# Turning the identity on TensorE where it stands idle, in a hybrid encoder kernel

## The chip, the cores and the metric

The kernel runs on one core of a Trainium2 chip (trn2). A core has a matrix engine, TensorE (PE; its weight loads are listed as PEld), VectorE (DVE), ScalarE (ACT), GpSimd (POOL) and SyncE (SP), which issues most transfers; each takes its own queue of instructions in order, and they meet through semaphores. SBUF is the on-chip memory, PSUM (8 banks of 512 fp32 columns on 128 partitions) takes what TensorE computes. The metric is device microseconds of one execution.

## The reference

Two encoder layers on 1024 tokens of 1024 channels, all in float32, batch 1.

```
x = (1, 1024, 1024)
layer 0: hn = rms_norm(x, g0); u = hn @ ev_w_in            # 1024 x 3072
         y_att = differential attention (4 heads, q/k norm, partial rotary) of u[:, :1536]
         y_hy  = order-2 Hyena of u[:, 1536:]  (3-tap conv, long filters by FFT, gating)
         x = x + concat(y_att, y_hy) @ ev_w_out
layer 1: u = rms_norm(x, g1) @ od_w_in                     # q, k, v, o, gates
         y = bidirectional chunkwise mLSTM (4 heads, chunks of 128), rms_norm, * sigmoid(o)
         x = x + y @ od_w_out
each layer: xt = rms_norm(x, gf)
         top-1 of 4 groups, top-2 of 8 experts in it;  32 experts, d_expert 512
         x = x + sum over picked e of gate * (silu(xt @ w1[e]) * (xt @ w3[e])) @ w2[e]
```

## The kernel before, in words

The program is a row of phases, each a block in which every engine has its own instruction list; at the end of a phase all engines meet at a barrier (`end_phase`), so nothing of the next phase starts before all of them are through. In order: `first_norm` (normalise x, turn it into xnT), `attention_project`, `attention`, `hyena_project`, `hyena_filter`, `hyena_transform`, `out_route` of layer 0 (output projection, residual, norm, router), `experts`, `overflow`, `renorm`, `ml_project_qk`, `ml_project_vo`, `ml_gates`, `ml_scan`, `out_route` of layer 1, `experts`, `overflow`.

Large products run as three fp32r products, high x high, high x rest and rest x high (`split_product`, lines 193 to 195): ScalarE casts the high part, VectorE subtracts it to get the rest (`rest_of`, line 188). Weights come in chunks of 2 MB through a ring of three slots; a phase finds its first chunks already there. So at the start of a projection phase TensorE first waits for these splits: `attention_project` for x and the first half of a weight chunk (waits on `x_rest` and `w_rest`), `hyena_project` and `ml_project_qk` for a 128-column weight block and a quarter of x, `out_route` for a quarter of w and half of y. Then it runs through tiles of 128 tokens (or blocks of 128 columns) with 8 contraction steps each.

`hyena_filter` has two small fp32 products of the filter network (line 1510) and four turnings (line 1520) per round, eight rounds; VectorE multiplies each result with a decay (lines 1584, 1586) that ScalarE computes, and its chain goes on to a sum that GpSimd gathers. Its first products need nothing that is computed in the phase.

`out_route` (line 658) is built once per layer. In layer 1 (`hs` is given) TensorE first turns the normalised mLSTM output (`turn_y`, line 849): the first half, then, when VectorE has read it (`y_rest`), the second; in layer 0 `turn_y` does nothing. After the last tile, `logits(NT - 1)`, the router's selection is a long chain on VectorE (lines 1129 to 1226) with two short parts on TensorE in it: a count of places, nine products that wait for `picked` and release `placed` (lines 905, 908), and sixteen products that write the list of tokens per block, wait for `marked` in two halves of eight and release `listed` (line 916). VectorE reads the lists (line 1224), GpSimd then gathers the first two blocks of tokens by an indirect transfer (line 831).

`experts` (line 1833) runs over the 32 experts, one block of 128 tokens each. For a block, TensorE turns the gathered tokens (`turn_x`, line 2002, eight turnings into banks 0 and 1), ScalarE casts them (`xgH`, line 2071), VectorE subtracts (`xgL`, line 2119), and only then does `one(e)` begin its products (lines 1985 to 1993). On ScalarE the order is written out: first half of the first weight chunk, the cast of the turned tokens, then the next halves; VectorE follows it. A ring slot is refilled when VectorE has made both rests of its chunk.

`renorm` (line 2316) loads x again, normalises each tile of 128 tokens on ScalarE and VectorE and turns it (line 2399).

Of the kernel before, what the change touches and what calls it, by code (L numbers as in the profile page):

```python
# [14 lines left out]
P = 128  # L15
# [56 lines left out]
def build(nc, I, out):  # L72
    ctx = ExitStack()
    with ctx:
# [111 lines left out]
        def rest_of(out, whole, high):  # L186

            return nc.vector.tensor_tensor(out, whole, high.bitcast(F32), ALU.subtract)  # L188

        def split_product(dst, lhs, rhs, start, stop):  # L190


            nc.tensor.matmul(dst, lhs[0], rhs[0], start=start, stop=False)  # L193
            nc.tensor.matmul(dst, lhs[0], rhs[1], start=False, stop=False)  # L194
            return nc.tensor.matmul(dst, lhs[1], rhs[0], start=False, stop=stop)  # L195
# [87 lines left out]
        def attention_project(q, kH, kL, v):  # L283
# [3 lines left out]
            with ExitStack() as st:  # L287
# [15 lines left out]
                with nc.Block() as block:  # L303
# [8 lines left out]
                    @block.tensor  # L312
                    def _(pe):
                        def turn(i):
                            pe.wait_ge(normed, i + 1)
                            if i >= 2:
                                pe.wait_ge(qk_moved, i - 1)
                            if i >= NT + 2:
                                pe.wait_ge(k_rest, i - NT - 1)
                            for h in range(AH):  # L320
                                last = nc.tensor.transpose(psum[:, 4 + i % 2, h * P:(h + 1) * P],
                                                           qn[:, i % 3, h * P:(h + 1) * P], ident[:])
                            last.then_inc(turned, 1)

                        for i in range(3 * NT):
                            c, j = divmod(i, NT)
                            pe.wait_ge(x_rest, i + 1)
                            if i >= 4:
                                if i - 4 < STEPS:
                                    pe.wait_ge(qk_read, i - 3)  # L330
                                else:
                                    pe.wait_ge(v_copied, i - 3 - STEPS)
                            for k in range(KD):
                                if j == 0 and k % 4 == 0:
                                    pe.wait_ge(w_rest, 2 * c + k // 4 + 1)
                                last = split_product(psum[:, i % 4, :], (xH[:, i % 2, k, :], xL[:, i % 2, k, :]),
                                                     (wH[:, c % 2, k, :], wide_rest(S_ATT + c)[:, k, :]),
                                                     k == 0, k == KD - 1)
                            last.then_inc(proj, 1)
                            if 2 <= i <= STEPS + 1:  # L340
                                turn(i - 2)
# [316 lines left out]
        def out_route(name, yT, hs, head_gain, s0, xsrc, xdst, layer, slots, slot_gate, ctrl, xg):  # L658
# [6 lines left out]
            with ExitStack() as st:  # L665
# [103 lines left out]
                with nc.Block() as block:  # L769
# [68 lines left out]
                    def _(pe):  # L838
# [38 lines left out]
                        def logits(j):  # L877
# [7 lines left out]
                                                        start=(k == 0), stop=(k == KD - 1))  # L885
                            last.then_inc(logit_ok, 1)

                        turn_y(0, 0)
                        turn_y(0, 1)
                        for j in range(NT):  # L890
                            project(j, 0)
                            turn_y(j + 1, 0)
                            if j:
                                turn_x(j - 1)
                            project(j, 1)
                            turn_y(j + 1, 1)
                            if j:
                                logits(j - 1)
# [2 lines left out]

                        pe.wait_ge(picked, 1)
                        nc.tensor.matmul(psum[:, PB, 0:(NT + 1) * NE], upperR[:], both[:].rearrange("p j e -> p (j e)"),
                                         start=True, stop=False)
# [3 lines left out]
                                                    start=False, stop=(j == NT - 1))  # L910
                        last.then_inc(placed, 1)

                        for n in range(16):
                            if n % 8 == 0:
                                pe.wait_ge(marked, n // 8 + 1)
                            last = nc.tensor.matmul(psum[:, SB, 0:3 * NBLKP], A[:, n, :],
                                                    B[:, n, :, :].rearrange("p f b -> p (f b)"),
                                                    start=(n == 0), stop=(n == 15))
                        last.then_inc(listed, 1)

                    @block.scalar
                    def _(act):
# [308 lines left out]
        def hyena_project(z, yT, xnH, o, gain, post, hidden, consts):  # L1231
# [4 lines left out]
            with ExitStack() as st:  # L1236
# [40 lines left out]
                with nc.Block() as block:  # L1277
# [12 lines left out]
                    def _(pe):  # L1290
# [9 lines left out]
                        def hidden_layer(u):  # L1300
# [4 lines left out]
                            else:  # L1305
# [3 lines left out]
                            nc.tensor.matmul(psum[:, TURN + u % 2, :], w[:], x[:, piece(u)], start=True, stop=True  # L1309
                                             ).then_inc(lin, 1)  # L1310

                        for i in range(STEPS):
                            pe.wait_ge(w_rest, i + 1)
                            if i >= 3:
                                pe.wait_ge(padded, i - 2)
                            for half in range(2):
                                ts = slice(half * 512, (half + 1) * 512)
                                for k in range(KD):
                                    if i == 0 and k % 4 == 0:
                                        pe.wait_ge(x_rest, 2 * half + k // 4 + 1)  # L1320
                                    last = split_product(psum[:, 2 * (i % 3) + half, :],
                                                         (wH[:, i % 2, k, :], block_of(wide_rest, i)[:, k, :]),
                                                         (xnH[:, k, ts], xnL[:, k, ts]), k == 0, k == KD - 1)
                            last.then_inc(proj, 1)
                            if i < NT:
                                turn(i)
                            if MLP <= i < MLP + 4:
                                hidden_layer(i - MLP)
# [153 lines left out]
        def hyena_filter(z, zT, hidden, consts, hs, hd, hinv, tab):  # L1482
# [4 lines left out]
            with ExitStack() as st:  # L1487
# [6 lines left out]
                with nc.Block() as block:  # L1494
# [7 lines left out]
                    def _(pe):  # L1502
# [11 lines left out]
                        def turn(n):  # L1514
# [6 lines left out]
                                                           z[:, ct, t0:t0 + 4 * P - 3:4], ident[:])  # L1521
                            last.then_inc(turned, 1)

                        for n in range(NT):
                            filters(n)
                            turn(n)
# [306 lines left out]
        def experts(layer, slots, slot_gate, ctrl, total, xg, y, yidx, oidx, w_over):  # L1833
# [6 lines left out]
            with ExitStack() as st:  # L1840
# [50 lines left out]
                with nc.Block() as block:  # L1891
# [85 lines left out]
                    def _(pe):  # L1977
# [63 lines left out]
                        def tail():  # L2041
                            turn_hid(LAST)
                            out(0, LAST, LAST + 1, 0)

                        turn_x(0, 0, 0)
                        for e in range(4):
                            one(e // 2, e % 2, e)
                        with pe.Fori(2, NE // 2 - 1) as i:
# [267 lines left out]
        def renorm(src, gain):  # L2316
# [3 lines left out]
            with ExitStack() as st:  # L2320
# [6 lines left out]
                with nc.Block() as block:  # L2327
                    @block.sync
                    def _(sp):
                        for j in range(NT):  # L2330
                            sp.dma_start(x_all[:, j, :], rows[:, j, :]).then_inc(x_in[j], 16)
                            if j == 0:
                                sp.dma_start(g_bc[:], gain.partition_broadcast(P)).then_inc(gain_in, 16)
# [56 lines left out]

                    @block.tensor
                    def _(pe):
                        for j in range(NT):
                            pe.wait_ge(xn_ok, j + 1)
                            if j >= 4:
# [33 lines left out]
        def ml_project_qk(qkT, G, xnH):  # L2429
# [3 lines left out]
            with ExitStack() as st:  # L2433
# [19 lines left out]
                with nc.Block() as block:  # L2453
# [6 lines left out]

                    @block.tensor
                    def _(pe):
                        for i in range(CONV):
                            pe.wait_ge(w_rest, i + 1)
                            if i >= 4:
# [689 lines left out]
```

## Time and profile before

| | us |
|---|---|
| median of 3 runs | 2720.84 (2719.23 to 2721.32) |
| profiled execution, its own time | 2724.51 |
| its span, first to last instruction | 2722.5 |
| TensorE busy | 2428.2 (89%), 11788 matrix instructions |
| VectorE busy | 1827.1 (67%) |
| ScalarE busy | 1452.7 (53%) |
| GpSimd busy | 483.5 (18%) |
| mean granted TensorE clock | 0.938 |

The profile is of one execution. Busy shares are means over phases with different limits, so each phase has to be read by itself. The granted clock is given as a share of full speed, 2.4 GHz; 0.50 is the lower of its two levels, 1.2 GHz.

### The profile page before, as it was taken

To read this page: it belongs to the slowest core of one execution; us is meant where nothing else is said; L and a number is where in the kernel's file an instruction comes from. 1 tells how busy PE (TensorE), PEld (TensorE's weight loads), DVE (VectorE), ACT (ScalarE), POOL (GpSimd) and SP (SyncE) were. 2 spreads that over 40 slices of the span, in tenths; PEclk is the share of its full clock that TensorE was granted. 3 is DMA by queue.
4 is the path that set the end of the run, shared out by engine and by line. 5 is a ranking of instruction groups with operands and counts; after the bars stand their busy time and mean duration, and the time that the engine had idled before them with its cause. 6 is when DMAs were issued, how large, how long until landed. Compare 5 with 4: busy or idle time off the path is not lost. (4 is left out here: it accounts for less than half of the span.)

```text
span 2722.5 us, 32997 instructions
## 1 busy us (share of the span) xinstructions
PE 2428.2 (89%) x11788; PEld 1995.0 (73%) x11788; DVE 1827.1 (67%) x2083; ACT 1452.7 (53%) x1776; POOL 483.5 (18%) x433
## 2 busy tenths in 40 slices
PE   5989989796959999999948999779695999999995
PEld 4768877585857888888836888667584888888882
DVE  5748856578358998899835301078546988888980
ACT  4337842322227887788834212146423778887870
POOL 0001100100002332333200000025200323332310
PEclk9999999897979999999978999979796999999997
DMA  4010011101339999999980101200424999999994
GB/s 171 31 64 1 1 39 42 70 31 36 117 115 344 389 385 381 382 389 391 373 327 22 50 31 64 91 1 1 144 109 170 387 367 380 369 387 380 395 375 167
DMA packets 85787, 542.51 MB, mean 199 GB/s; under 512 B 18870, under 2 KB 22551, under 8 KB 59704
## 3 DMA queue, kind: packets, MB, share of 16 engines
q1 hardware_dynamic: 64232, 503.11, 47.0%
q0 software_dynamic: 19008, 33.61, 5.1%
q10 hardware_dynamic: 2448, 4.46, 0.4%
q8 instruction: 63, 1.03, 0.2%
q14 instruction: 36, 0.29, 0.0%
HBM read 521.70 MB, written 55.05 MB: 212 GB/s over the span
## 5 line engine op out<-in xcount | busy, mean ns | idle before, releaser
L2119 DVE TENSOR_TENSOR wL<-ring,wH 128x2048 fp32r<-128x2048 f32 x384 | 869.1, 2288 | 153.7 <-ACT wH L2066 148.4
L2066 ACT CAST wH<-ring 128x2048 fp32r<-128x2048 f32 x384 | 730.3, 1910 | 216.6 <-DMA ring<-in_moe_w 158.8
L1985 PE MATMUL psum<-wH,xgH 128*128 128x512 f32 x1024 | 408.0, 398 | 14.0 <-DVE xgL L2119 13.9
L1987 PE MATMUL psum<-wH,xgL 128*128 128x512 f32 x1024 | 401.3, 392 | 0.0
L1993 PE MATMUL psum<-wL,xgH 128*128 128x512 f32 x1024 | 275.4, 391 | 0.0
L1985 PEld LDWEIGHTS psum<-wH,xgH 128*128 128x128 f32 x1024 | 193.6, 189 | 57.3 <-DVE xgL L2119 13.0
L1993 PEld LDWEIGHTS psum<-wL,xgH 128*128 128x128 f32 x1024 | 193.0, 188 | 40.7
L1987 PEld LDWEIGHTS psum<-wH,xgL 128*128 128x128 f32 x1024 | 193.8, 189 | 38.4
L1985 PE MATMUL psum<-wH,hidH 128*128 128x512 f32 x512 | 207.8, 406 | 11.0 <-DVE hidL L2119 11.0
L1987 PE MATMUL psum<-wH,hidL 128*128 128x512 f32 x512 | 201.6, 394 | 0.0
L1932 POOL COPY gidx<-slots 128x1 int32 (+1 forms) x60 | 62.6, 1044 | 488.6 <-PE psum L2002 488.6
L1993 PE MATMUL psum<-wL,hidH 128*128 128x512 f32 x512 | 138.0, 392 | 0.0
L195 PE MATMUL psum<-xn_high,ring_rest 128*128 128x512 f32 x320 | 126.7, 396 | 0.0
L1985 PEld LDWEIGHTS psum<-wH,hidH 128*128 128x128 f32 x512 | 97.5, 190 | 30.5 <-DVE hidL L2119 11.4
L1993 PEld LDWEIGHTS psum<-wL,hidH 128*128 128x128 f32 x512 | 97.1, 190 | 20.4
L1987 PEld LDWEIGHTS psum<-wH,hidL 128*128 128x128 f32 x512 | 97.7, 191 | 18.5
L193 PE MATMUL psum<-w_high_route_rest,y_high_route 128*128 128x512 f32 x256 | 104.5, 408 | 7.0 <-DVE ring_rest L188 7.0
L193 PE MATMUL psum<-w_high_vo,xn_high 128*128 128x512 f32 x256 | 102.1, 399 | 3.6 <-DVE ring_rest L188 3.6
L195 PE MATMUL psum<-w_high_vo,xnT_rest 128*128 128x512 f32 x256 | 101.9, 398 | 0.0
L194 PE MATMUL psum<-ring_rest,xn_high 128*128 128x512 f32 x256 | 101.6, 397 | 0.0
L194 PE MATMUL psum<-ring_rest,y_high_route 128*128 128x512 f32 x256 | 101.4, 396 | 0.0
L195 PE MATMUL psum<-w_high_route_rest,y_rest_route 128*128 128x512 f32 x256 | 101.4, 396 | 0.0
(425 smaller groups left out, 4728.9 us busy)
## 6 DMA issues: line engine op xcount, KB each, us to landing
ring<-in_moe_w SPq DMA_DIRECT2D x192, 2048.0 KB, 9.4
ring<-in_ev_w_in SPq DMA_DIRECT2D x6, 2048.0 KB, 14.7
xnT<-in_moe_w SPq DMA_DIRECT2D x6, 2048.0 KB, 13.8
ring<-in_od_w_in SPq DMA_DIRECT2D x6, 2048.0 KB, 15.4
xn_scratch<-xn_route SPq DMA_DIRECT2D x16, 512.0 KB, 2.6
ow<-in_moe_w SPq DMA_DIRECT2D x3, 2048.0 KB, 22.6
x_all<-in_x SPq DMA_DIRECT2D x4, 1024.0 KB, 8.1
ring<-in_ev_w_out SPq DMA_DIRECT2D x2, 2048.0 KB, 7.8
```

Source lines behind the costliest of these rows:

```text
L193: nc.tensor.matmul(dst, lhs[0], rhs[0], start=start, stop=False)
L194: nc.tensor.matmul(dst, lhs[0], rhs[1], start=False, stop=False)
L195: return nc.tensor.matmul(dst, lhs[1], rhs[0], start=False, stop=stop)
L1932: nc.gpsimd.tensor_copy(idx[:, b:b + 1], slots[:, bass.ds(e, 1)]).then_inc(idx_ok, 1)
L1985: nc.tensor.matmul(psum[:, bank, :], xh[:, k, :], w3[0][:, n, cols], start=(half == 0 and n == 0), stop=False)
L1987: nc.tensor.matmul(psum[:, bank, :], xl[:, k, :], w3[0][:, n, cols], start=False, stop=False)
L1993: ins = nc.tensor.matmul(psum[:, bank, :], xh[:, k, :], w3[1][:, n, cols], start=False, stop=(half == 1 and n == len(ks) - 1))
L2066: nc.scalar.copy(half_of(wH, b, e, c, half), raw(e, c, half)).then_inc(w_high, 1)
L2119: return nc.vector.tensor_tensor(out, whole, high.bitcast(F32), ALU.subtract)
```

## The change

A new helper, `idle_products(bank, n)`, turns the 128x128 identity n times into the first 128 columns of a PSUM bank. Nothing reads the result. It has no semaphore, and n is fixed when the program is built. It is called at twelve lines of TensorE's lists; two of them are inside `experts` and three in `out_route` that both layers run, so an execution passes eighteen calls with 869 turnings in all: one each of 55 (`attention_project`), 52 (`hyena_project`), 30 (`hyena_filter`), 50 (`renorm`) and 55 (`ml_project_qk`); 45 and 26 in each `experts`; in `out_route` 52 (layer 0) or 120 and 45 (layer 1), and in both layers 50, 72 and 12. Nothing is removed or moved.

```
+        def idle_products(bank, n):
+
+            for _ in range(n):
+                nc.tensor.transpose(psum[:, bank, 0:P], ident[:], ident[:])

@@ attention_project
+                        idle_products(7, 55)
                         for i in range(3 * NT):
@@ out_route
+                        idle_products(3, 52 if hs is None else 120)
                         turn_y(0, 0)
                         turn_y(0, 1)
+                        if hs is not None:
+                            idle_products(3, 45)
                         for j in range(NT):
                             project(j, 0)
...
+                        idle_products(3, 50)
                         pe.wait_ge(picked, 1)
...
                         last.then_inc(placed, 1)

+                        idle_products(3, 72)
                         for n in range(16):
...
                         last.then_inc(listed, 1)
+                        idle_products(3, 12)
@@ hyena_project
+                        idle_products(7, 52)
                         for i in range(STEPS):
@@ hyena_filter
+                        idle_products(7, 30)
                         for n in range(NT):
                             filters(n)
@@ experts
+                        idle_products(7, 45)
                         turn_x(0, 0, 0)
+                        idle_products(7, 26)
                         for e in range(4):
                             one(e // 2, e % 2, e)
@@ renorm
+                        idle_products(7, 50)
                         for j in range(NT):
@@ ml_project_qk
+                        idle_products(7, 55)
                         for i in range(CONV):
```

## Rows read from the trace of the kernel before

**Rows 1.** The page, parts 1 (PE alone) and 2 (TensorE's clock, tenths in 40 slices).
```profile
PE 2428.2 (89%) x11788; PEld 1995.0 (73%) x11788; DVE 1827.1 (67%) x2083; ACT 1452.7 (53%) x1776; POOL 483.5 (18%) x433
...
PEclk9999999897979999999978999979796999999997
```

**Rows 2.** Stretches at four stage starts: start:end, us, PE busy, granted clock, DMA.
```profile
34.81:40.13 5.32, 0.00 (x1) 0.50 0.12 32
40.13:44.70 4.57, 4.57 (x11) 0.50 0.03 9
349.55:354.87 5.32, 0.00 (x1) 0.72 0.46 129
354.87:358.72 3.85, 3.85 (x9) 0.50 0.24 82
663.84:666.81 2.97, 0.00 (x0) 0.50 0.68 210
666.81:672.74 5.93, 5.93 (x14) 0.50 1.00 246
1441.49:1446.81 5.32, 0.00 (x0) 0.50 0.37 114
1446.81:1450.98 4.17, 4.17 (x10) 0.50 0.00 0
...
348.22:349.55 1.33, 0.00 (x0) 1.00 0.00 0
```

**Rows 3.** First norm: one line's durations (min/median/max ns); timeline (start, us, count).
```profile
L273 PE MATMUL psum<-ident,x_all x64: 272/273/476, 19.1 to 32.9; 128*128 128x128 f32 x64
...
19.13 3.65 PE L273 MATMUL psum<-ident,x_all 128*128 128x128 f32 x16 [19.13 <-DVE x_all L257]
...
23.04 1.64 PE L273 MATMUL psum<-ident,x_all 128*128 128x128 f32 x8 [0.27 <-DVE x_all L257]
...
24.84 1.09 PE L273 MATMUL psum<-ident,x_all 128*128 128x128 f32 x8 [0.15 <-DVE x_all L257]
```

**Rows 4.** Start of the experts: timeline of layer 0, slow stretches of both layers.
```profile
810.36 1.94 PE L2002 MATMUL psum<-ident,xg 128*128 128x128 f32 x8 [7.70 <-PEq L105]
...
815.81 0.80 PE L1985 MATMUL psum<-wH,xgH 128*128 128x512 f32 x1 [3.51 <-DVE xgL L2119]
...
815.81:819.52 3.71, 3.71 (x9) 0.50 0.61 138
2086.75:2092.70 5.95, 5.95 (x14) 0.50 0.67 191
```

**Rows 5.** Sum of forty stretches of 5 us, 1000 to 1200, inside the first experts.
```profile
sum 200.00, PE 199.21 PEld 165.23 DVE 177.92 ACT 158.93 POOL 66.23; mean PE 4.98 PEld 4.13 DVE 4.45 ACT 3.97 POOL 1.66
```

**Rows 6.** Start of layer 1's out_route: PE's stretches and a timeline row.
```profile
1911.51:1923.52 12.01, 0.00 (x1) 0.50 0.88 288
1932.29:1935.68 3.39, 3.39 (x10) 0.50 0.32 124
...
1930.79 0.68 DVE L188 TENSOR_TENSOR y_rest_route<-psum,y_high_route 128x512 fp32r<-128x512 f32 x1
```

**Rows 7.** Start of hyena_filter, timeline.
```profile
504.01 2.10 PE L1510 MATMUL psum<-hy_w,hy_hidden 64*128 64x512 f32 x4 [5.50 <-PEq L105]
...
509.16 0.69 DVE L1584 TENSOR_TENSOR xnT<-psum,hy_decay 128x512 f32<-128x512 f32 x1 [1.74 <-PE psum L1510]
```

**Rows 8.** The router's selection in layer 0: PE's stretches and a timeline row.
```profile
780.61:787.59 6.98, 0.00 (x0) 0.50 1.02 383
789.72:798.98 9.26, 0.00 (x1) 0.50 0.03 11
...
802.70 0.21 DVE L1224 TENSOR_SCALAR slots<-psum 128x48 int32<-128x48 f32 x1 [1.05 <-PE psum L916]
```

**Rows 9.** PE's stretches: start of renorm, end of the router.
```profile
1411.43:1423.56 12.13, 0.00 (x0) 0.50 0.84 329
802.67:810.36 7.69, 0.00 (x0) 0.50 0.25 68
```

More of the change, by code:

```diff
@@ L188, in rest_of, with idle_products @@
             return nc.vector.tensor_tensor(out, whole, high.bitcast(F32), ALU.subtract)
+        def idle_products(bank, n):
+            for _ in range(n):
+                nc.tensor.transpose(psum[:, bank, 0:P], ident[:], ident[:])
         def split_product(dst, lhs, rhs, start, stop):
@@ L323, in turn @@
                             last.then_inc(turned, 1)
+                        idle_products(7, 55)
                         for i in range(3 * NT):
@@ L886, in logits @@
                             last.then_inc(logit_ok, 1)
+                        idle_products(3, 52 if hs is None else 120)
                         turn_y(0, 0)
                         turn_y(0, 1)
+                        if hs is not None:
+                            idle_products(3, 45)
                         for j in range(NT):
@@ L900, in _ @@
                         logits(NT - 1)
+                        idle_products(3, 50)
                         pe.wait_ge(picked, 1)
@@ L911, in _ @@
                         last.then_inc(placed, 1)
+                        idle_products(3, 72)
                         for n in range(16):
@@ L919, in _ @@
                         last.then_inc(listed, 1)
+                        idle_products(3, 12)
                     @block.scalar
@@ L1310, in hidden_layer @@
                                              ).then_inc(lin, 1)
+                        idle_products(7, 52)
                         for i in range(STEPS):
@@ L1522, in turn @@
                             last.then_inc(turned, 1)
+                        idle_products(7, 30)
                         for n in range(NT):
@@ L2043, in tail @@
                             out(0, LAST, LAST + 1, 0)
+                        idle_products(7, 45)
                         turn_x(0, 0, 0)
+                        idle_products(7, 26)
                         for e in range(4):
@@ L2392, in _ @@
                     def _(pe):
+                        idle_products(7, 50)
                         for j in range(NT):
@@ L2462, in _ @@
                     def _(pe):
+                        idle_products(7, 55)
                         for i in range(CONV):
```

## The prediction

> **What bounds the kernel now.** The page's first two parts come first [rows 1]: TensorE (PE) is busy 89% of the span, and its granted clock is at 0.9 or more in most of the 40 slices and at 0.7 in a few. The next view is the table of stretches, cut at each stage: it shows that low slices are stage starts. In [rows 2] each stage that opens with fp32r products has the same two halves. For 2.97 to 5.32 us the engine has nothing to do, since ScalarE and VectorE still split the first operands; the products then run at granted clock 0.50 (1.2 of the two levels, 1.2 and 2.4 GHz) for 3.85 to 5.93 us before the clock goes to 1.00. In these stages PE is busy without a gap afterwards, so a microsecond of products at the low clock costs half a microsecond of the total. The reader should see both numbers side by side: the idle time is the cover that the new work has, half of the slow time is all that it can win. The expert loops are also PE's: 199.21 of 200 us busy in the middle of the first [rows 5]. The router's selection is VectorE's chain, with PE idle for 6.98 and 9.26 us inside it [rows 8].
>
> **What one added operation costs.** The change only adds: 869 transposes of the identity over an execution, waiting for nothing, in order ahead of the stage's own work on PE's queue. Whatever stands behind them on that queue waits until they are done. The trace has the same form, a 128x128 fp32 transpose against the identity, in the first norm [rows 3]. Slow: 16 took 3.65 us with 0.476 for a single one, so one follows another after (3.65 - 0.476)/15 = 0.212 us. Fast: 8 took 1.09 with 0.272 for one, so (1.09 - 0.272)/7 = 0.117 us. These lengths also decide what the clock did there: the page gives 1.00 for the first norm, but the first 16 have the slow length and the later ones the fast one. So transposes alone raise the clock, here between 23.04 and 24.84 us, some 4 to 5.7 us after they began. (The Trainium skill says otherwise: "TensorE: Matmul & The Clock Gate", section "PE-mode transpose", holds that the full clock does not engage for them. The trace disagrees, with 0.476 against 0.272 us; by that rule the change would have nothing but cost, and that is a rival below.)
>
> How long N of them take: the slow phase of the six stage starts in [rows 2, 4] is 4.57, 3.85, 5.93, 4.17, 3.71 and 5.95, mean 4.7 us. That is 22 transposes at 0.212, the rest at 0.117: D(55) = 8.6, D(52) = 8.2, D(50) = 8.0, D(45) = 7.4, D(30) = 5.6 us. With the clock up from the start it is 0.117 N. The cover is often shorter than that.
>
> **Part by part.** Net cost = what overruns the cover, less half of the slow stretch.
> - attention_project, 55: 8.6 - 5.32 = 3.3 late, half of 4.57 won: +1.0 us. If the clock does not fall between the stages: 6.4 - 5.32 - 2.3 = -1.2.
> - ml_project_qk, 55: 8.6 - 5.32 - 2.1 = +1.2 (other end -1.0).
> - hyena_project, 52: here the clock is still 1.00 when the stage begins, 1.33 us after the last product [rows 2], and it fell only in the long pause that the transposes now fill. So 6.1 - 5.32 - 1.9 = -1.1 (other end: 8.2, +1.0).
> - out_route of layer 0, 52: cover only 2.97. 8.2 - 2.97 - 2.97 = +2.3 (other end +0.2).
> - experts, 45 before the first turning and 26 after it, in both layers: PE starts together with the others at 810.36, with its operand landed, so there is no cover at all for the 45 [rows 4]. ScalarE's copy of the turned operand waits for it, behind that its next weight casts, and behind those VectorE's. First product after 7.4 + 8 x 0.117 + 26 x 0.117 = 11.4 us where it was 815.81 - 810.36 = 5.45: 5.95 late; won 1.86 and 2.98. +4.1 and +3.0, together +7.1. The loop behind it is PE's [rows 5] and takes over the delay. Ends: 5.3 for the 45 gives +2.9 in all; if the refill of the ring, which hangs on the later casts, counted rather than PE, up to 7 each.
> - out_route of layer 1, 120 and 45: 120 take 4.7 + 98 x 0.117 = 16.2 us against 12.01 idle; but the result of the first turning is read by VectorE only at 1930.79 [rows 6], and 1911.51 + 16.2 + 0.5 = 1928.2 is before that. Hidden; if that cover were gone, 4.2. The 45 after the second turning have none: the first product followed it at once. 5.3 to 7.4 us, depending on whether the clock lasted over the pause before; I take the middle, 6.4, less half of 3.39: +4.7.
> - hyena_filter, 30: the first product comes with the stage, again no cover. Two rounds ended at 509.16, 5.15 us after the start and at the low clock [rows 7]; at the high one they are half. 5.6 + 2.6 - 5.15 = +3.1; behind them VectorE's chain starts late by that (ends +0.9 and +4).
> - Router, both layers: 50 against 6.98 idle, 8.0 - 6.98 = 1.0 late; the nine small products behind them filled 787.59 to 789.72, 2.1 us at the low clock, and win that back. 72 at 0.117 = 8.4 fit into 9.26. The 16 list products then end sooner, and the 1.05 us that VectorE waits for them at the end [rows 8] goes: -1.05 twice, -2.1. What is late next is VectorE itself. If the clock falls in between: 4.7 + 50 x 0.117 = 10.5, 1.3 late: +0.2 each.
> - renorm, 50, under 12.13 us of waiting for data, and the 12 at the router's end under 7.69 [rows 9]: 0. Without cover they would be 8.0 and 1.4 to 2.5 each. The pause that is left behind renorm's 50 is 4 us, so I count on no gain for its own transposes (at most 1 us).
>
> Sum: 1.0 + 1.2 - 1.1 + 2.3 + 7.1 + 4.7 + 3.1 - 2.1 = +16.2 us. The profiled execution took 2724.51 us (span 2722.5, 2.0 around it), 3.7 above the median; against it the changed one would be 2740.7, and in terms of the median 2720.84 + 16.2 = 2737.0.
>
> **The rivals.**
> (a) Faster: two transposes of one and the same operand follow each other quicker than those of fresh data, say a load of weights hidden under the last product, at half the distance, 0.106 and 0.0585. Then D(N) = 2.35 + 0.0585 N: 5.6 for 55, 5.0 for 45. Same working: -2.0, -1.9 (both projections), -1.9 (hyena), -0.6, experts 5.0 + 0.9 + 1.5 - 5.45 = 2.0 late, so +0.1 and -1.0, layer-1 route +2.1, filter +1.5, router -2.1: -5.8, 2715. The sum changes sign at about 0.073 us for one at the high clock. For it: the small covers at the projections would just fit. Against it: all transposes that the trace shows have 0.117. 11%.
> (b) The clock stays up over the pauses between stages, since PE is now idle for 1 to 2 us there only: 0.117 N everywhere. -1.2, -1.0, -1.1, +0.2, +2.9, 5.3 - 1.7 = +3.6, +0.9, -2.1: +2.2, 2723. For it: 1.33 us did not lower it; against it: at most of the ten starts it is 0.50 already when the stage begins. 10%.
> (c) The transposes don't raise the clock: 0.212 N, nothing won. 6.3 + 5.7 + 6.3 + 8.0, experts 9.5 + 1.9 + 5.5 - 5.45 = 11.5 twice, layer-1 route 16, filter 6.4, router (3.6 + 6.0) twice: +91, 2812. Against it: [rows 3]. 4%.
> (d) The experts' end is set by the stream of weights and their late start is absorbed: 16.2 - 7.1 = +9, 2730. Against it: PE has 0.4% of idle time in that stretch. 10%.
>
> **How the numbers follow.** Forecast 2737, 62%, its own range 2728 to 2746 from the ends above; 3% for none of these. 2717 to 2749 leaves out (a), (c) and part of the tails, some 2 in 10. Faster or slower by 0.2% is 5.4 us, about what a measurement can tell from no change: (a) lies on that edge, with more favourable ends 8% are below 2715.4; (b), part of (a) and the low end of (d) make 15% within; 77% slower.
>
> **What would show it.** In the changed profile: the added operations stand 0.21, then 0.117 us apart (0.106 and 0.06 for (a)); first products in attention_project at 43 instead of 40.13, in out_route of layer 0 some 5 us later in its stage, the first experts' product 11.4 us behind the stage's start and at clock 1.00; VectorE's wait of 1.05 us for the lists gone. Wrong would be: products at 0.50 after the transposes, or no overrun, or an expert loop whose end does not move with its start.

## The result and the profile after

The changed kernel took 2732.37 us (median of 8 runs, 2726.89 to 2736.69), the kernel before on the same chip 2721.08 us (2719.23 to 2724.61): a ratio of 1.0039, 95% interval 1.0027 to 1.0051, or +11.3 us. Run again beside other kernels in a later series it gave 2727.05 us and 1.0018 (1.0009 to 1.0026), +5.4 us. Slower both times; on record were 2737 us and +16.2 us. Both results are inside the stated 2717 to 2749 us, the second a little below the forecast's own range of 2728 to 2746, and the forecast was 5 and 11 us too much.

Parts 1 (busy time of each engine) and 2 (TensorE's busy share in tenths, and its clock, in 40 slices) of the page of after, against [rows 1]:

```profile
PE 2515.0 (92%) x12657; PEld 2088.3 (76%) x12657; DVE 1827.8 (67%) x2083; ACT 1451.4 (53%) x1776; POOL 468.8 (17%) x433
...
PE   6989999796989999999969999779898999999995
...
PEclk9999999898999999999979999979999999999998
...
L193 PE MATMUL psum<-ident 128*128 128x128 f32 x869 | 121.4, 311 | 46.6 <-PEq L105 46.6
```

The last row is from part 5: the 869 turnings are busy for 121.4 us, and each call starts as soon as TensorE's list comes to it. The clock rose as meant (mean 0.961 instead of 0.938, of 2.4 GHz), TensorE's busy share went from 89 to 92%, and the span grew from 2722.5 to 2731.4 us.

The calls at six stages, in the timeline of after (start, us, engine, line, operation, count; in brackets the wait before), against [rows 2, 4, 6, 7]:

```profile
34.82 6.19 PE L193 MATMUL psum<-ident 128*128 128x128 f32 x55 [1.71 <-PEq L105]
40.77 0.48 PE L198 MATMUL psum<-w_high_qk,x_high_qk 128*128 128x512 f32 x1
...
497.69 6.22 PE L193 MATMUL psum<-ident 128*128 128x128 f32 x30 [5.51 <-PEq L105]
503.84 1.25 PE L1523 MATMUL psum<-hy_w,hy_hidden 64*128 64x512 f32 x4
505.14 0.69 DVE L1598 TENSOR_TENSOR xnT<-psum,hy_decay 128x512 f32<-128x512 f32 x1 [8.42 <-PE psum L1523]
...
507.00 0.69 DVE L1598 TENSOR_TENSOR xnT<-psum,hy_decay 128x512 f32<-128x512 f32 x1 [0.57 <-PE psum L1523]
...
661.70 8.54 PE L193 MATMUL psum<-ident 128*128 128x128 f32 x52 [4.03 <-PEq L105]
670.00 0.47 PE L198 MATMUL psum<-w_high_route_rest,y_high_route 128*128 128x512 f32 x1
...
808.58 7.73 PE L193 MATMUL psum<-ident 128*128 128x128 f32 x45 [5.44 <-PEq L105]
816.14 1.04 PE L2016 MATMUL psum<-ident,xg 128*128 128x128 f32 x8
816.78 1.07 ACT L2087 CAST xgH<-psum 128x512 fp32r<-128x512 f32 x2 [6.33 <-PE psum L2016]
817.02 3.00 PE L193 MATMUL psum<-ident 128*128 128x128 f32 x26
...
819.78 0.47 PE L1999 MATMUL psum<-wH,xgH 128*128 128x512 f32 x1
...
1442.77 9.16 PE L193 MATMUL psum<-ident 128*128 128x128 f32 x55 [1.70 <-PEq L105]
1451.68 0.48 PE L198 MATMUL psum<-xn_high,w_high_ml 128*128 128x512 f32 x1
...
1915.92 15.22 PE L193 MATMUL psum<-ident 128*128 128x128 f32 x120 [4.31 <-PEq L105]
...
1936.38 6.74 PE L193 MATMUL psum<-ident 128*128 128x128 f32 x45
1942.88 0.48 PE L198 MATMUL psum<-w_high_route_rest,y_high_route 128*128 128x512 f32 x1
```

All first products behind calls now take 0.47 or 0.48 us, a full-clock length, where [rows 4] has 0.80. And nearly all of them start the moment the last turning ends: the engine still turns the identity when the operands are already there. That is the overrun. The 55 turnings took 6.19 us at the first stage and 9.16 us at ml_project_qk; the same list of operations has two lengths.

Stage lengths, from the first instruction of each stage to that of the next, for the profiled executions of before, after, and after again (its span 8.4 us shorter than the first), with the term on record:

| stage | before | after | again | change, on record | change, seen |
|---|---|---|---|---|---|
| attention_project | 155.15 | 152.27 | 152.24 | +1.0 | -2.9, -2.9 |
| attention | 159.58 | 157.51 | 157.83 | 0 | -2.1, -1.8 |
| hyena_project | 154.44 | 153.08 | 153.07 | -1.1 | -1.4, -1.4 |
| hyena_filter | 30.33 | 34.49 | 34.52 | +3.1 | +4.2, +4.2 |
| out_route and router, layer 0 | 146.50 | 146.88 | 147.04 | +1.25 | +0.4, +0.5 |
| experts, layer 0 | 601.09 | 604.41 | 601.95 | +4.1 | +3.3, +0.9 |
| ml_project (to the gates) | 312.02 | 314.58 | 312.97 | +1.2 | +2.6, +1.0 |
| out_route and router, layer 1 | 169.80 | 171.55 | 167.75 | +3.65 | +1.8, -2.1 |
| experts, layer 1, to the end | 641.22 | 643.98 | 642.22 | +3.0 | +2.8, +1.0 |

The stages left out changed by 1.5 us or less. The -2.9 and -2.1 of the first two rows are not the calls' work alone: two test kernels with nothing changed in these two stages have them 2 us shorter each as well (experiment 2). A stage of one execution is not a measurement: the last one, whose beginning was as before in four of the test kernels below (the one with the router's calls, with the three uncovered ones, with the three large ones, with attention_project's alone), had 644.30, 639.03, 641.36 and 641.90 us there. For sizes the timed series below count.

### The profile page after: what moved, and what is told of

Its sections match the earlier page's. It is cut to its first block and busy times, and to the rows that moved or that the text cites. A ratio compares the mean times of both kernels' runs of the same rounds, so it can differ in the third digit from the quotient of the medians.

```text
span 2731.4 us, 34735 instructions
## 1 busy us (share of the span) xinstructions
PE 2515.0 (92%) x12657; PEld 2088.3 (76%) x12657; DVE 1827.8 (67%) x2083; ACT 1451.4 (53%) x1776; POOL 468.8 (17%) x433
## 5 line engine op out<-in xcount | busy, mean ns | idle before, releaser
L2135 DVE TENSOR_TENSOR wL<-ring,wH 128x2048 fp32r<-128x2048 f32 x384 | 869.5, 2288 | 153.0 <-ACT wH L2082 148.5
L193 PE MATMUL psum<-ident 128*128 128x128 f32 x869 | 121.4, 311 | 46.6 <-PEq L105 46.6
L193 PEld LDWEIGHTS psum<-ident 128*128 128x128 f32 x869 | 117.9, 164 | 49.3 <-issue 49.3
L1946 POOL COPY gidx<-slots 128x1 int32 (+1 forms) x60 | 49.8, 829 | 494.9 <-PE psum L2016 494.9
L1999 PEld LDWEIGHTS psum<-wH,hidH 128*128 128x128 f32 x512 | 97.6, 191 | 30.4 <-DVE hidL L2135 11.3
```

Of the source, the lines that this page charges most:

```text
L193: nc.tensor.transpose(psum[:, bank, 0:P], ident[:], ident[:])
L1946: nc.gpsimd.tensor_copy(idx[:, b:b + 1], slots[:, bass.ds(e, 1)]).then_inc(idx_ok, 1)
L1999: nc.tensor.matmul(psum[:, bank, :], xh[:, k, :], w3[0][:, n, cols], start=(half == 0 and n == 0), stop=False)
```

## Experiments

Twelve test runs were made, two of them repeats, in three series, each beside runs of the kernel before on its chip (medians 2721.36, 2721.66 and 2720.99 us). In the expectations attproj is attention_project, and x4_fitted the kernel of experiment 9. The theory is the sum of the prediction: a call costs what it overruns its cover and wins half of the slow stretch.

**1. The change without the experts' calls**

```
-                        idle_products(7, 45)
                         turn_x(0, 0, 0)
-                        idle_products(7, 26)
```

> The change without its two calls in experts (45 and 26 left out, both layers); all other calls stay. Theory (the turnings have no cover there and the expert loop is TensorE's, so the late start is passed on): in both profiles of before and after the experts' first product moved from 5.45 to 11.4 us and 10.3 us behind the stage's start, so the time falls by about 7 us against the change, to 2725, ratio to before 1.0015. Rival (the stream of weights sets the end of the experts and absorbs the late start): no change, 2732, ratio 1.004.

Measured: 2722.30 us, ratio 1.0001 (0.9989 to 1.0013). (The trace of after has the first products 11.2 and 10.1 us behind the stage's start.) Against the first series of the change, 1.0039 (1.0027 to 1.0051), the experts' calls cost more than nothing; against its second, 1.0018 (1.0009 to 1.0026), the intervals overlap, so this run alone does not show it. It does show that what is left costs less than on record: the other terms, +9.1 together on record, are within 3.5 us of nothing.

**2. The experts' calls alone**, in both layers, in the kernel before

```
+                        idle_products(7, 45)
                         turn_x(0, 0, 0)
+                        idle_products(7, 26)
```

> The kernel before with only the change's two calls in experts (45 before the first turning, 26 after it). Theory: +7 us over before (4.1 and 3.0, bounds 3 and 8), ratio 1.0026, and the whole of each experts stage longer by 3 to 4 us, from its first instruction to the next stage's. Rival (absorbed): 0, ratio 1.000.

Measured: 2725.65 us, ratio 1.0016 (1.0003 to 1.0029), so +4.4 us where the sum has +7.1. The delay is real. Its profiled execution spans 2722.6 us, no longer than before, with the stages 605.17 and 642.89 (before 601.09 and 641.22) but attention_project and attention each 2 us shorter though nothing in them was changed. One profile would have hidden the cost. What makes those two shorter can be seen in one stretch of attention_project, first of before, then of this kernel (start:end, length, PE busy, granted clock, DMA share, GB/s):

```profile
109.55:112.96 3.41, 3.22 (x10) 0.50 0.00 0
...
109.53:112.94 3.41, 3.41 (x18) 1.00 0.00 0
```

At the same place the clock was down in one execution and up in the other, with 10 and 18 products done. The fourteen profiled executions fall into two groups: in eight the clock goes down near 109 us and attention takes 159.5 to 159.7 us (before among them), in six it does not and attention takes 157.2 to 157.8 (after and after again among them, this kernel and that of experiment 5, where no call stands in or before these stages). The kernel of experiment 9 is in one group the first time and in the other the second time.

**3. The same with a longer first call**

```
-                        idle_products(7, 45)
+                        idle_products(7, 90)
                         turn_x(0, 0, 0)
```

> The kernel with the experts' calls alone (45 and 26), the 45 made 90. Theory (the first product is late by every added transpose, at 0.117 us each once the clock is up, and nothing later absorbs it): 45 x 0.117 = 5.3 us in each layer, +10.5 us over the kernel with 45, so 2736 and a ratio near 1.0055. Rival (the experts' weights come by DMA and a late start is won back behind it): the same as with 45, a ratio of 1.0016.

Measured: 2738.82 us, ratio 1.0063 (1.0050 to 1.0076), 12.8 us (give or take 5) above the kernel with 45. Layer 0 in the timelines of the two, first 45, then 90:

```profile
805.44 8.07 PE L193 MATMUL psum<-ident 128*128 128x128 f32 x45 [7.38 <-PEq L105]
...
816.98 0.48 PE L1992 MATMUL psum<-wH,xgH 128*128 128x512 f32 x1
```

```profile
811.15 12.86 PE L193 MATMUL psum<-ident 128*128 128x128 f32 x90 [7.61 <-PEq L105]
...
827.48 0.47 PE L1992 MATMUL psum<-wH,xgH 128*128 128x512 f32 x1
```

45 more turnings are 4.79 us more, 0.106 each on average, and the first product goes from 11.54 to 16.33 us behind the stage's start; in layer 1 from 10.98 to 15.83. That is 9.6 us over both, inside the interval of 7.8 to 17.8 us by which the total grew. The rival in which the stream of weights absorbs a late start is out. (In the two single profiles the experts' stages differ by 3.5 and 2.0 us only, 608.66 and 644.92 against 605.17 and 642.89; what took up the rest there was not followed.)

**4. The router's calls alone**, in both layers, in the kernel before

```
+                        idle_products(3, 50)
                         pe.wait_ge(picked, 1)
...
+                        idle_products(3, 72)
                         for n in range(16):
...
                         last.then_inc(listed, 1)
+                        idle_products(3, 12)
```

> The kernel before with only the router's calls (50, 72 and 12, both layers). Theory: the list products end sooner, VectorE's wait of 1.05 us for them goes, in each layer; the 50 are 1 us late and the nine products win it back: -2.1 us in all, 2719, ratio 0.9992; bounds -2.1 and +0.4. Rival (the late 50 and the gap between the calls cost more than is won): VectorE waits over 1 us longer for the places, +1 to +3 us, ratio 1.0007.

Measured: 2721.33 us, ratio 1.0003 (0.9992 to 1.0014): +0.8 us, from -2.2 to +3.8. Nothing that can be measured, in either direction. The mechanism itself is there. VectorE's write of the lists in after, which in [rows 8] waited 1.05 us, waits no more:

```profile
800.85 0.20 DVE L1236 TENSOR_SCALAR slots<-psum 128x48 int32<-128x48 f32 x1
```

and in the router-only kernel the two stages that hold a router are 144.81 and 168.37 us, 1.7 and 1.4 less than before. These 3 us are at the edge of what the series can tell, and its last stage happened to be 3.1 us longer.

**5. The uncovered calls outside the experts alone**, in the kernel before

```
+                        idle_products(3, 52 if hs is None else 0)
                         turn_y(0, 0)
                         turn_y(0, 1)
+                        if hs is not None:
+                            idle_products(3, 45)
...
+                        idle_products(7, 30)
                         for n in range(NT):
                             filters(n)
```

> The kernel before with three calls alone, those outside the experts for which the terms of the sum were late starts: 30 at hyena_filter, 52 at the start of the first out_route, and in the second out_route 45 behind the turning (no 120 ahead of it). Theory of the sum (a run of calls that outlasts its cover delays the stage, and half of the slow stretch comes back): +3.1 +2.3 +4.7 = +10, so 2731.5 and a ratio near 1.0037. In the change's own trace the hyena_filter stage is 4.2 us longer than before. Rival (the calls fill time in which TensorE would have waited anyway): +3 at most, a ratio of 1.001 or less.

Measured: 2726.29 us, ratio 1.0020 (1.0010 to 1.0029): +5.4 us (2.7 to 7.9) instead of +10.1. They cost, about half as much. Its stages that hold them are 3.6, 1.8 and 3.7 us longer than before, together 9.1, close to the sum; but hyena_transform (behind hyena_filter, unchanged) was 3.5 us shorter, and 9.1 - 3.5 = 5.6 us is what the timed runs have. The whole stage in before, in this kernel and in that of experiment 6, then one stretch of it in before and the same one, 32.67 us behind the stage's start, in this kernel (start:end, length, PE busy, granted clock, DMA share, GB/s):

```profile
534.26:663.82 129.56, 105.87 (x448) 0.88 0.05 17
...
533.13:659.16 126.03, 102.37 (x448) 0.91 0.06 17
...
531.51:658.82 127.31, 103.65 (x448) 0.89 0.05 17
...
566.93:573.76 6.83, 5.87 (x14) 0.50 0.92 301
...
565.80:572.63 6.83, 6.13 (x28) 1.00 0.88 290
```

The same 448 operations keep TensorE busy for 105.87, 102.37 and 103.65 us, and in all three it is idle for 23.7 us. So the difference is the clock: it was down over the stretch in before, with 14 operations done, and up in this kernel, with 28. The stage took 129.4 to 129.7 us in eight profiled executions and 125.6 to 127.4 in six. The six have calls at just one of hyena_project and hyena_filter; the eight have calls at neither (five) or at both (three, the change among them). As far as fourteen executions show it, calls move the clock's ups and downs in a later stage that they do not touch. Why both together leave the long form is open, and no timed run has this effect by itself.

**6. The three large calls alone**, in the kernel before

```
+                        idle_products(7, 55)
                         for i in range(3 * NT):
...
+                        idle_products(7, 52)
                         for i in range(STEPS):
...
+                        idle_products(7, 55)
                         for i in range(CONV):
```

> The kernel before with the three large covered calls alone: 55 at attproj, 52 at hyena_project, 55 at ml_project_qk. The sum has +1.0 -1.1 +1.2 = +1.1, so 2722.5 and a ratio of 1.0004, within 0.999 to 1.001. If the clock has not fallen when attproj's calls start, as in the change's own trace (0.110 us each from the first), that call gives about 3 us more back than the sum has: 2719, 0.9992. Rival (the calls outlast their cover by their whole slow length in all three places): +7 or more, a ratio of 1.0026.

Measured: 2716.53 us, ratio 0.9977 (0.9967 to 0.9987): -6.3 us (-9.0 to -3.5), outside the +1.1 of the sum. These are the terms that failed. At attention_project and ml_project_qk the clock was still up when this kernel's calls began. Stretches of before, of after and of the three-call kernel (start:end, length, PE busy, weight loads, VectorE, ScalarE, GpSimd, granted clock, DMA share, GB/s):

```profile
34.00:34.80 0.80, 0.00 (x0) 0.00 (x0) 0.00 (x0) 0.00 (x0) 0.00 (x0) 0.79 0.00 0
34.80:36.00 1.20, 0.00 (x0) 0.00 (x0) 0.11 (x1) 1.19 (x2) 0.00 (x0) 0.50 0.02 5
```

```profile
34.00:34.80 0.80, 0.00 (x0) 0.01 (x1) 0.00 (x0) 0.01 (x1) 0.00 (x0) 1.00 0.00 0
34.80:36.00 1.20, 1.18 (x11) 1.20 (x12) 0.13 (x1) 1.20 (x2) 0.00 (x0) 1.00 0.02 5
...
1442.77:1451.68 8.91, 8.91 (x55) 8.91 (x56) 7.28 (x4) 8.91 (x6) 0.00 (x0) 0.66 0.24 70
```

```profile
1434.35:1440.35 6.00, 5.96 (x56) 5.99 (x56) 4.32 (x3) 5.98 (x4) 0.00 (x0) 1.00 0.32 101
```

Up to 34.80 us before and after issue the same instructions. In before the clock fell inside the 1.7 us pause there, in after it did not. ml_project_qk shows both as well: 0.66 over after's calls, 1.00 over those of the three-call kernel. At one and the same place the same pause sometimes takes the clock down and sometimes not. Besides, hyena_transform is 2.25 us shorter here than in before (127.31 against 129.56, rows in experiment 5), a stage for which the sum had nothing.

**7. attention_project's call alone**, in the kernel before

```
+                        idle_products(7, 55)
                         for i in range(3 * NT):
```

> The kernel before with the 55 calls at attproj alone. The sum on record has +1.0 for it (all 55 at the slow pace at first, first product at 43). In the change's own trace the clock never fell, the first product stands at 40.8 and the products behind it run at 0.39: then it gives 4.6 - 0.6 = 4 us back, of which its stage shows 1.5 to 2.9: a ratio of 0.9985 to 0.9995. Rival (the term of the sum): 1.0004.

Measured: 2720.28 us, ratio 1.0002 (0.9986 to 1.0018). The first product stood at 40.81 us at full clock and the stage was 1.3 us shorter (153.82), but in the total neither the -2 to -4 expected nor the +1.0 on record can be told from nothing. How the 6.3 us of experiment 6 are shared out, no timed run says; hyena_transform, shorter there, had its long form here (129.59 us).

**8. The change once more**

> The change itself once more, on the chip and beside the runs of the kernels sent with it, so that its parts can be added up against it: 2732, a ratio of 1.004. The terms found so far are +4.3 for the experts (45 and 26 alone) and nothing for the router's calls; if parts add up, the three calls outside the experts and the three large ones together must give the other 7 us.

Measured: 2727.05 us, ratio 1.0018 (1.0009 to 1.0026). The parts: +4.4 (experts), +0.8 (router), +5.4 (uncovered), -6.3 (large) sum to +4.3 us, against +5.4 for the whole. They add up within their intervals, though the first series of the change had 11.3. Why that one was higher is open; the profiled executions show a difference of the kind. In layer 1's out_route the second one has

```profile
1928.60:1930.97 2.37, 0.00 (x1) 0.01 (x1) 2.28 (x6) 0.58 (x1) 0.69 (x1) 1.00 0.06 21
1931.46:1936.29 4.83, 4.83 (x47) 4.83 (x46) 3.10 (x3) 4.31 (x13) 3.56 (x2) 1.00 0.28 102
```

and the first one

```profile
1930.98:1935.89 4.91, 0.60 (x7) 0.36 (x5) 4.82 (x7) 0.59 (x1) 2.46 (x1) 1.00 0.06 23
1936.38:1942.88 6.50, 6.50 (x48) 6.50 (x46) 4.77 (x4) 5.98 (x14) 2.37 (x1) 0.74 0.19 74
```

The first row of each is the pause, the second the 45 calls. In the second execution the operand came 2.1 us earlier (the pause ends 1930.97 - 1913.07 = 17.90 us behind the first call instead of 1935.89 - 1915.92 = 19.97), the clock was up throughout, and the calls took 4.83 us. In the first the pause was 4.31 us (the 0.60 us busy at its head is the first turning); its row still says 1.00, but over the calls the clock is 0.74, and they took 6.50. The two stages differ by 2.1 + 1.7 = 3.8 us, of one and the same kernel. The earlier operand need not be the calls' doing: the kernel of experiment 7, which has no call in this stage, has its first product 18.7 us behind the stage's start, before 20.8.

**9. Calls cut to their cover**

```
attention_project 55 -> 25      out_route layer 0   52 -> 14
hyena_project     52 -> 40      out_route layer 1   120, 45 -> 28 between the two turnings
hyena_filter      30 -> 0       router  50, 72, 12 -> 36, 72, 12
experts       45, 26 -> 0, 16   renorm 50 -> 0
ml_project_qk     55 -> 25
```

> Counts cut to the cover that the trace of before shows, at 0.212 us each: attention_project and ml_project_qk 25, hyena_project 40, out_route of layer 0 14, in layer 1 none at the start and none after the second turning but 28 between the two turnings, router 36, 72 and 12, experts none before and 16 after the turning, none in hyena_filter and renorm. Theory (what costs is the overrun, what is won is half of the slow stretch): 1.9 + 1.9 + 1.8 + 1.3 + 1.2 + 2.1 + 2.8 = 13 us won, 2708, ratio 0.995, and faster than both kernels. Rival (the clock falls again before the products, or its slow stretches are not on the path): within 3 us of before, ratio 0.999 to 1.000.

Measured: 2702.85 us, ratio 0.9931 (0.9913 to 0.9948). It beats both kernels, and by more than the 13 us expected: -18.8 us (-23.7 to -14.2). Part of the rest is hyena_transform, for which the sum had nothing; it is 4.0 us shorter than before in this profile and 2.3 in the next one. Once more, in the third series:

> The fitted kernel of x4_fitted once more, unchanged: 0.993 of the kernel before if the gain holds on another day's chip, 0.998 or more if it was luck of one series.

Measured: 2701.63 us, ratio 0.9937 (0.9914 to 0.9959). Experts, layer 0, in the first of these kernels:

```profile
799.52 1.94 PE L2017 MATMUL psum<-ident,xg 128*128 128x128 f32 x8 [6.87 <-PEq L105]
801.26 3.62 PE L193 MATMUL psum<-ident 128*128 128x128 f32 x16
804.98 0.67 PE L2000 MATMUL psum<-wH,xgH 128*128 128x512 f32 x1
805.48 0.40 PE L2002 MATMUL psum<-wH,xgL 128*128 128x512 f32 x1
```

The first product stands 5.46 us behind the start of the stage, as before (5.45), and the next ones run at 0.40 instead of 0.63 us. Nothing is late, and the slow stretch is gone: in this profile the two experts' stages are 3.3 and 0.4 us shorter than before.

**10. That kernel without the experts' 16**

> The fitted kernel without its 16 calls between the experts' turning and their first product. Theory: in either layer the first products run slow again (0.63 instead of 0.39 us for about 3.5 us, half of it lost) and the 16 calls were covered, so +1.5 to +2 us per layer, +3 to +4 in all: 0.9945. Rival (the weights' DMA has slack that absorbs the experts' start): equal to the fitted kernel.

Measured: 2706.33 us, ratio 0.9950 (0.9930 to 0.9969). The point moved as expected, by 4.7 us of median or 3.5 by the ratios, but the intervals overlap. The slow stretch is back:

```profile
802.14 0.79 PE L2000 MATMUL psum<-wH,xgH 128*128 128x512 f32 x1 [3.51 <-DVE xgL L2134]
802.73 0.63 PE L2002 MATMUL psum<-wH,xgL 128*128 128x512 f32 x1
```

**11. That kernel with the three large calls back at 55, 52 and 55**

> The fitted kernel (x4_fitted) with its three large calls back at the change's length: 55 instead of 25 at attproj, 52 instead of 40 at hyena_project, 55 instead of 25 at ml_project_qk. Theory of the sum (what lies beyond the cover is a late start): 55 warm calls at attproj end 0.6 us past the cover but keep the clock up over the first products, where the 25 leave 4.6 us at the slow pace; ml_project_qk: 55 are 3 us beyond the cover if the clock is down at their start, hidden if it is up. Net -4 to +2 us on 2702.9: a ratio of 0.9915 to 0.994. Rival (cover is all that counts, so every call beyond it costs): +6, 0.9955.

Measured: 2705.07 us, ratio 0.9947 (0.9927 to 0.9967), between the two and not to be told from the fitted kernel. This time the clock was down when the first calls began, and they overran by 2.1 us (42.27 against 40.13 in before):

```profile
34.82:42.27 7.45, 7.45 (x55) 7.45 (x56) 5.82 (x4) 7.45 (x6) 0.00 (x0) 0.79 0.13 29
42.27:46.00 3.73, 3.73 (x19) 3.07 (x18) 3.73 (x3) 1.74 (x1) 0.00 (x0) 1.00 0.00 0
```

The short call has the other risk. In the first fitted execution its 25 turnings ran at full clock from 34.82 to 37.74, and the 2.37 us left of the pause were enough for the clock to be down again soon after the products had begun:

```profile
37.74:40.11 2.37, 0.00 (x1) 0.03 (x1) 2.37 (x2) 2.37 (x2) 0.00 (x0) 1.00 0.26 65
40.11:46.00 5.89, 5.89 (x19) 4.66 (x20) 5.89 (x4) 3.87 (x3) 0.00 (x0) 0.71 0.01 3
```

Its stage was 154.67 us long; in the repeat, where the 25 started near the clock's fall and took 4.58 us, 151.59. About half of these 3.1 us is the start. The other half is the fall near 109 us (experiment 2), which the first of the two executions has and the second has not.

## Why the prediction was right and wrong

**Right: direction, mechanism and the largest term.** Calls stand in order ahead of real work, so they cost their overrun. Of the marks named, three stand nearly to the digit: the pace of 0.21, then 0.11 us per turning (0.117 on record); the experts' first product 11.2 us behind the stage's start (11.4 on record) at full clock; layer 0's out_route 8.3 us behind its start instead of 2.97, 5.3 later (5 on record). VectorE's wait for the lists is gone. One mark failed: the first product of attention_project was to stand at 43 us and stands at 40.77. Experiments 2 and 3 show that the experts' late start stays in the total: +4.4 us (0.8 to 7.9) against +7.1. That the number came within 5 us the first time is in part luck: the parts measured by themselves sum to +4.3 us, and the second series has +5.4.

**Rivals.** (a) half the pace: out, the turnings are 0.109 to 0.110 us apart at full clock. (c) turnings do not raise the clock: out, by the 0.40 us products behind the 16 turnings of experiment 9 and the 0.63 us without them in experiment 10, and by after, where the 0.48 us first products stand directly behind the turnings. The Trainium skill has the contrary rule ("TensorE: Matmul & The Clock Gate", section "PE-mode transpose"); no run here bears it out. (d) absorbed: out, by experiment 3. (b) the clock stays up over the pauses: true at some stage starts in some executions, and that is what the sum lacked.

**The step that failed: one state of the clock per stage start.** The prediction read 0.50 in the pauses of [rows 2], an execution that it took for all of them, and gave attention_project and ml_project_qk D(55) = 8.6 us. Nine profiled executions have calls at attention_project. The clock was up when they began in five (55 of them took 6.2 us, 25 took 2.9) and down, or fell just then, in four (55 took 7.7 us, 25 took 4.6). At ml_project_qk it was up in two of eight. With the clock up, the prediction's own working has 5.95 - 5.32 - 2.3 = -1.7 us for attention_project and 5.96 - 5.32 - 2.1 = -1.5 for ml_project_qk; with hyena_project's -1.1, where the clock had been taken as up and was in all eight executions (its stages -1.4), that makes -4.3 us, inside the interval of experiment 6, where the +1.1 on record is outside. These three terms are 7.4 of the 11.9 us between the 16.2 on record and the 4.3 that the parts sum to.

The stages bear this out only when like is compared with like. In the group of executions with the clock's fall near 109 us (experiment 2), attention_project took 155.2 to 155.5 us without calls, 153.7 and 153.8 with 55 calls and the clock up, and 155.2 and 155.3 with 55 calls and the clock down; in the other group it took 153.0 and 153.2 without calls and 152.2 and 152.3 with 55 and the clock up. So the call is worth some -1.4 or -0.8 us with the clock up and nothing with it down, and the rest of the table's -2.9 is not its work. For ml_project_qk the -2.1 of the three-call kernel is no clean measure either: without calls the stage had 117.6 to 119.2 us, with them 116.8 there.

**A length that was mis-sized.** Even where the clock was down, D(55) = 8.6 us was mostly too long: the first product stood 7.4 to 7.9 us behind the first call in five of the six stage starts with 55 calls and the clock down, and 8.9 in the sixth. With 7.45 the working gives 7.45 - 5.32 - 2.3 = -0.2 us for attention_project, where +1.0 was on record.

**A term put at nothing: stages without calls.** The sum has nothing for stages that the calls do not touch. hyena_transform is 2.25 us shorter in the kernel of experiment 6 and 3.5 us in that of experiment 5, by TensorE's clock alone. With it the three large calls come to -4.3 - 2.25 = -6.5 us where -6.3 was measured, and the three uncovered ones to 9.1 - 3.5 = 5.6 where 5.4 was. That rests on profiles of one execution each. In the change itself the stage has its old length.

**Terms mis-sized.** The three uncovered calls: +5.4 us instead of +10.1, though their own stages are 9.1 us longer in the profile; the difference is hyena_transform's, as said. hyena_filter was on record with +3.1 and shows +3.6 to +4.3. In after it is found in the two terms of the sum: the 30 turnings took 503.84 - 497.69 = 6.15 us instead of 5.6, and the two rounds behind them 507.00 - 503.84 = 3.16 instead of 2.6, so the second round's result reaches VectorE 9.31 us behind the stage's start instead of 5.15, 4.2 late. Layer 1's 45 were put midway between 5.3 and 7.4 us of turning, at 6.4; the two executions had 4.8 and 6.5. The router's -2.1 is neither shown nor refuted (-2.2 to +3.8).

**Hidden terms.** The second turning of layer 1's out_route ends its wait at 1935.89 - 1915.92 = 19.97 us behind the first call, 20.01 (1931.52 - 1911.51) in before: the 120 cost nothing there, as on record. Neither they nor renorm's 50 were tried by themselves; renorm took 29.8 and 31.5 us in the two executions of the change and 30.1 in before, and 31.9 in a kernel without calls there (experiment 11).

## What to carry to other kernels

Filling idle time of TensorE to keep its clock costs what the filling overruns the arrival of the next real operand and wins half of the slow stretch: here calls of full length cost 0.2 to 0.4%, and the same idea with every call cut to its cover gave 0.63 to 0.69% back. An overrun of well under the prize does no harm (the large calls overran by 0.3 to 0.6 us in experiment 6, which gained 6.3). Take both from the trace, the idle time as the budget and half of the slow stretch as the prize, and put the calls between the first dependent step and the wait behind it, not ahead of the step (experts: 16 behind the turning cost nothing, 45 ahead of it delay every cast). Where a stage's clock was read from one execution, work the term out for both clock states, since the total moved by several microseconds between executions of one kernel. And before a stage's change of length is put down to an edit, compare TensorE's busy time for the same number of operations: where that differs, the clock did it, perhaps in a stage that the edit does not touch.

## What was not expected of the hardware

A pause of 1.7 us on TensorE, with the same instructions before it, brought the granted clock down in some executions (0.79 over 34.00 to 34.80 us in before) and not in others (1.00 in after). Where it was down, turnings brought it back while they ran (0.79 as the mean over the 55 of experiment 11). The Trainium skill ("TensorE: Matmul & The Clock Gate", section "Part 1: The HAM clock gate (the "warmup" mystery)") says that the number of slow matmuls of one kernel varies from run to run; the trace agrees for turnings, with 9.16 and 7.76 us for the same 55 at ml_project_qk in two executions of the change.

A 128x128 fp32 turning of one and the same operand follows the last in 0.109 to 0.110 us at full clock ((3.00 - 0.272)/25 and (6.19 - 0.272)/54), a little faster than the 0.117 of [rows 3].
